# A decoder of two layers with routed experts: GpSimd makes the low halves of every fourth expert weight chunk

## The reference

```python
wg = w_gate.transpose(1, 0, 2).reshape(D, N_EXPERTS * EXPERT_HIDDEN)
wu = w_up.transpose(1, 0, 2).reshape(D, N_EXPERTS * EXPERT_HIDDEN)
wd = w_down.reshape(N_EXPERTS * EXPERT_HIDDEN, D)
h = jax.nn.silu(xc @ wg) * (xc @ wu)
h = (h.reshape(-1, N_EXPERTS, EXPERT_HIDDEN) * gc[..., None]).reshape(-1, N_EXPERTS * EXPERT_HIDDEN)
return h @ wd
```

## Time and profile before

| | |
|---|---|
| median of three runs | 2354.69 us |
| the profiled execution | 2358.64 us |
| its span (first to last instruction) | 2356.8 us |
| mean granted TensorE clock | 0.967 |
| first expert part (rows of experts 4 to 15) | 1436 to 1757 us |
| second expert part | 2016 to 2337 us |

### The profile page before, as it was taken

How to read it: one execution, slowest core, us unless ns; L and a number is a source line. 1 busy time by engine, 2 the same in 40 slices (tenths; PEclk the granted TensorE clock), 3 DMA queues, 4 the chain that set the end, 5 groups by cost and what they waited for, 6 DMA issues and landing times.

```text
span 2356.8 us, 36755 instructions
## 1 busy us (share of the span) xinstructions
PE 2232.4 (95%) x13894; PEld 1884.3 (80%) x13894; DVE 1489.5 (63%) x2333; ACT 1090.4 (46%) x1557; POOL 240.1 (10%) x241
## 2 busy tenths in 40 slices
PE   8999999999999999899999889999999898999997
PEld 6877667999787866799976579887888577888786
DVE  2946355755394635675534577888765267788876
ACT  1142452444114244244433355676654456666665
POOL 1914000100081400011000000000000000000000
PEclk9999899999999999999999889999999898999999
DMA  4432113555343221356532236888855414688883
GB/s 159 146 119 82 63 63 126 177 183 172 122 143 117 81 68 67 136 187 197 183 130 90 72 128 214 309 299 311 295 195 179 143 46 152 237 308 301 306 295 134
DMA packets 109808, 396.86 MB, mean 168 GB/s; under 512 B 12088, under 2 KB 14144, under 8 KB 109376
## 3 DMA queue, kind: packets, MB, share of 16 engines
q1 hardware_dynamic: 108576, 393.45, 49.0%
q10 hardware_dynamic: 1056, 1.06, 0.1%
HBM read 393.40 MB, written 1.06 MB: 167 GB/s over the span
## 4 chain that ended last, share of the span: by engine, by line
PE 81%; DVE 13%; ACT 4%; issue 2%; DMA 1%; DVEq 0%; SPq 0%; ACTq 0%
PE psum L544 79%; DVE W_LO L1690 3%; PE psum L552 1%; DVE region L1695 1%; DVE region L1698 1%; DVE RS L1727 1%; ACT region L1243 1%; ACT W_HI L1238 1%; DVE SQ L1695 1%; ACT region L1247 0%; DMA ring<-in_weights 0%; ACT SQ L1243 0%; DMA PAR<-in_params 0%; ACT L1243 0%; DVE X_LO L1695 0%
## 5 line engine op out<-in xcount | busy, mean ns | idle before, releaser
L1690 DVE TENSOR_TENSOR W_LO<-ring,W_HI 128x1024 fp32r<-128x1024 f32 x435 | 533.0, 1225 | 218.6 <-ACT W_HI L1238 208.5
L1238 ACT ACTIVATE W_HI<-ring 128x1024 fp32r<-128x1024 f32 x435 | 461.8, 1062 | 325.1 <-PE psum L544 245.6
L544 PE MATMUL psum<-HN,ring 128*128 128x272 f32 (+1 forms) x1728 | 411.9, 399 | 9.7 <-DVE HN L1702 9.7
L544 PEld LDWEIGHTS psum<-HN,ring 128*128 128x128 f32 x1728 | 332.2, 194 | 82.1 <-issue 16.6
L544 PE MATMUL psum<-X_HI,W_HI 128*128 128x256 f32 x808 | 232.3, 287 | 8.1 <-DVE W_LO L1690 6.6
L544 PE MATMUL psum<-X_LO,W_HI 128*128 128x256 f32 x808 | 227.6, 282 | 0.0
L544 PE MATMUL psum<-X_HI,W_LO 128*128 128x256 f32 x808 | 227.4, 281 | 0.0
L1247 ACT ACTIVATE region<-psum 128x272 f32<-128x272 f32 (+10 forms) x227 | 89.6, 395 | 280.0 <-PE psum L544 258.7
L1690 DVE TENSOR_TENSOR W_LO<-SQ,W_HI 128x1024 fp32r<-128x1024 f32 x128 | 156.8, 1225 | 37.0 <-ACT W_HI L1238 32.9
L544 PE MATMUL psum<-W_HI,XG_HI 128*128 128x512 f32 x384 | 152.9, 398 | 17.3 <-DVE W_LO L1690 15.3
L544 PE MATMUL psum<-FN_HI,W_HI 128*128 128x272 f32 (+1 forms) x592 | 169.2, 286 | 0.0
(11 more groups left out here) (328 smaller groups left out, 4203.1 us busy)
## 6 DMA issues: line engine op xcount, KB each, us to landing
ring<-in_weights SPq DMA_DIRECT2D x615, 512.0 KB, 4.1
SQ<-in_weights SPq DMA_DIRECT2D x128, 512.0 KB, 4.8
XT<-in_x SPq DMA_DIRECT2D x1, 1088.0 KB, 5.1
CST<-in_consts SPq DMA_DIRECT2D x1, 1082.5 KB, 7.3
SQ<-bias_by_distance ACTq DMA_DIRECT2D x1, 1024.0 KB, 5.3
out<-XT SPq DMA_DIRECT2D x8, 128.0 KB, 1.9
PAR<-in_params SPq DMA_DIRECT2D x1, 572.0 KB, 8.2
bias_by_distance<-MIX ACTq DMA_DIRECT2D x1, 12.0 KB
```

What stands on the lines that cost most here:

```text
L544: ins = nc.tensor.matmul(dst, w, x, start=start, stop=stop, skip_group_check=True)
L1238: lane(nc.scalar.activation(W_HI[:, s % SPLIT, :], ring_slot(n), ACT.Copy), split_hi)
L1690: lane(nc.vector.tensor_tensor(W_LO[:, s % SPLIT, :], ring_slot(n), W_HI[:, s % SPLIT, :].bitcast(F32), ALU.subtract), split_lo)
```

## The change

In the two expert parts the low half of a chunk with c = 3 (every fourth: the last of gate, up and down of each of 16 experts, in two layers, 96 in all) is made by GpSimd, with the same subtraction. It reports on a semaphore of its own, `split_pool`. TensorE and SyncE wait for that one where a chunk is GpSimd's. VectorE leaves these chunks out and keeps the order of all else; ScalarE's part is as before. GpSimd goes through the expert steps with `abreast` in the same way, three chunks ahead, and has nothing else to do there. TensorE gets one more wait per layer: ahead of the first chunk of expert 4 it waits until the last gathered pair of banks has been read.

```diff
+        self.by_pool = []
...
-            def chunk(split=False, routed=None):
+            def chunk(split=False, routed=None, by_pool=False):
...
-                    pe.wait_ge(split_lo, i + 1)
+                    splits.by_pool.append(by_pool)
+                    pe.wait_ge(split_pool if by_pool else split_lo, splits.by_pool.count(by_pool))
...
-                return chunk(True, (l, e // GROUP, at + c))
+                return chunk(True, (l, e // GROUP, at + c), by_pool=(at + c) % 4 == 3)
...
                 w = expert_chunk(l, part, e, c)
+                if (part, e, c) == ("gate", GROUP, 0):
+                    for p in range(2):
+                        banks.await_read(pe, ("gathered", l, p, KT - 1))
...
             def split(s, n):
 
+                if splits.by_pool[s]:
+                    return
                 dve.wait_ge(split_hi, s + 1)
...
         def _(pool):
             lane = Lane(pool, sem("gpsimd_step"))
 
+            def split(s, n):
+
+                if not splits.by_pool[s]:
+                    return
+                pool.wait_ge(split_hi, s + 1)
+                lane(nc.gpsimd.tensor_tensor(W_LO[:, s % SPLIT, :], ring_slot(n), W_HI[:, s % SPLIT, :].bitcast(F32), ALU.subtract), split_pool)
+
+            follow = Follower(splits, split)
+
+            def abreast(l, step):
+
+                follow.to(min(splits.marks[step][0] + SPLIT - 1, splits.first["moe", l, "last"] + 1))
+
+            def moe_done(l):
+                follow.to(splits.first["moe", l, "last"] + 1)
+                follow.ceilings.pop(0)
...
             for name, *args in SCHEDULE:
-                if name in steps:
+                if name in ("moe_lead", "wide", "rows", "rows_turn", "rows_down", "wide_down"):
+                    abreast(args[0], ("step", name, *args))
+                elif name in steps:
                     steps[name](*args)
+                follow(("step", name, *args))
...
                 if splits.before[n] is not None:
-                    split_, count = rank[splits.before[n]]
-                    sp.wait_ge(split_lo if split_ else w_used, count)
+                    sp.wait_ge(*rank[splits.before[n]])
```

More of the change, by code:

```diff
@@ L515, in build_program @@
         arrived = [sem(f"weights_arrived{s}") for s in range(ROUTED_RING)]
-        w_used, split_hi, split_lo, split_used = (sem(n) for n in ("weights_used", "split_hi", "split_lo", "split_used"))
+        w_used, split_hi, split_lo, split_pool, split_used = (sem(n) for n in ("weights_used", "split_hi", "split_lo", "split_pool", "split_used"))
         splits = Splits()
@@ L2468, in load @@
                 sp.dma_start(ring_slot(n), stream[bass.ds(row, 128), :]).then_inc(arrived[splits.slot[n]], 16)
-            split_chunks = set(splits.chunks)
-            rank, counts = [], [0, 0]
+            maker = {n: split_pool if by_pool else split_lo for n, by_pool in zip(splits.chunks, splits.by_pool)}
+            rank, counts = [], {}
             for n in range(n_chunks):
-                counts[n in split_chunks] += 1
-                rank.append((n in split_chunks, counts[n in split_chunks]))
+                freed = maker.get(n, w_used)
+                counts[freed.name] = counts.get(freed.name, 0) + 1
+                rank.append((freed, counts[freed.name]))
             group_at, begin = {}, {}
```

## The result

The changed kernel takes 2380.19 us (median of nine runs, 2372.37 to 2384.86) against 2358.25 us of the kernel before in nine runs (2348.59 to 2366.28). The ratio is 1.0091, 95% interval 1.0072 to 1.0109: slower by 22 us. I had forecast 2352 us and a range to 2371, so the time lies outside it, and on the other side.

A forecast was written before the change was run, and what follows sets the result against it. TensorE, 95% busy, was taken to bound the kernel, low halves giving back at most 15 us. Two layers of -2.7 us gain plus 1.3 us gate cost gave -2.8 us, predicting 2352 us, range 2340 to 2371.

The forecast's parts named there:

- the price of GpSimd's subtraction: Each moved low half: GpSimd's plain 128 x 1024 subtraction taken as 1.95 us, between 1.82 and 2.88.
- the 0.13 us a gate: Last chunk of some 10 of 12 row gates: ready after 4.24 us, wanted after 4.11; 1.3 us a layer lost.
- VectorE is shut out: VectorE instructions with two SBUF inputs wait for GpSimd's whole instruction; PSUM readers run free; no 1.25 us gained per chunk.
- the waits at u5.2, g6.0, d10.0 and g12.0: TensorE in full stretches: u5.2 0.7 us late, g6.0 0.25 earlier, d10.0 as late as before, g12.0 at 1630.1 instead of 1631.06.
- The slope: Each 0.1 us on GpSimd's instruction moves the sum about 2.8 us: 10 gates and 4 full-stretch places, in two layers.
- margin of 1.1: VectorE's low half of a row chunk: made in 3.0 us, needed after 4.11, so 1.1 us to spare.
- Rival 1: GpSimd's instruction is longer, uncovered at g.3 of every row expert: at 2.35 us +8.4, 2363 us; chance 0.27.
- sign of being wrong, a minimum above 2.1 us: In the profile, a minimum above 2.1 us for GpSimd's subtraction would refute the forecast in favour of rival 1.
- Rival 3: GpSimd gets in ahead of TensorE's next chunk more often, some two more a layer: +8 us, 2360 us; chance 0.13.
- The gain of 2.7 us a layer in the full stretches: Where VectorE is full, TensorE waits less: 0.25 us at e = 5, 1.77 at e = 8, 0.7 at e = 11.
- The new wait at g4.0: First chunk of expert 4: costs nothing, since XG_LO is done at 1435.68 and TensorE waits for SGM until 1435.93 anyway.
- SyncE's later ring slots: Ring slots behind GpSimd's chunks come free 0.7 us later; cost nothing, as ScalarE hardly waits for landings.

## Why the prediction was wrong

- **The step that failed is the price of GpSimd's subtraction: 1.95 us, where it takes 2.41.** I drew a line through squares, which read one tile twice, and a subtraction with broadcast inputs, whose two inputs are views of one tile as well (`HB`, L2440). The kernel that reads one tile twice shows 1.89 us, so that line was right for such inputs and not for this one. The trace had a nearer row, the convolution's sum of two different tiles:

```profile
L2428 POOL TENSOR_TENSOR region<-region x60: 763/900/905, 56.0 to 704.9; 128x272 f32<-128x272 f32 x60
```

  0.763 us at 272 columns stands against 0.641 for the square of the same size. The prediction doesn't weigh it. With the 0.18 us that the squares' line has at no columns, 0.763 gives (0.763 - 0.18) x 1024 / 272 + 0.18, about 2.37 us, an estimate from rows of before; the runs show 2.41. The Trainium skill (GPSIMD Engine Reference, "3.1 Elementwise — side-by-side cycle accounting") gives 4497 ns for 2048 columns; half of it, the estimate of 2.25 us in the prediction, was nearer than the 1.95 I took.
- **Up to the length it assumed, the mechanism and the total hold.** For 1.95 us the prediction has -1.4 us a layer; at 1.96 us the part is 1.6 shorter, at 1.89 us (-2.2 by its slope) 2.3. That the total came so near is partly luck: 0.6 of the 1.6 us is the wide chunks' pace, and the 0.13 us a gate never came, since the row gate of before begins g.3 4.22 us after g.0, not 4.11 (its first chunk takes 1.47 us). With 816 columns g.3 of the gates begins 4.21 to 4.22 us after g.0 too. VectorE is shut out as foreseen, PSUM readers run free, and the waits at u5.2, g6.0, d10.0 and g12.0 stand where they were drawn (0.38, 0.65, 1.34 and 1.01 us shown at 1.89 us).
- **The slope was half of what it is, and that is the second step that failed.** I had 2.8 us per 0.1 us for both layers. From 1.96 to 2.41 us the two parts grow by 27.8 us, 6.2 per 0.1 (some 2.4 of the 27.8 us is the wide chunks' pace). At the row gates a length of 2.41 gives 2.04 + 0.14 + 2.41 + 0.05 = 4.64 us, 0.42 over the 4.22; g.3 begins after 4.63 us, and 0.12 more is lost behind it. But new places join in, which the prediction put at nothing. (Of the other row chunks it says that most have a wide chunk among the three before them; GpSimd's wide chunks it doesn't price at all.) Two GpSimd chunks in a row need more than the pace gives (three wide downs, 1.06 us each by the starts), VectorE's next chunk after a shut-out of 2.1 us misses its margin of 1.1 (d6.2 and d9.2, 1.16 each), u4.3 costs 0.55, and the second matmul of six wide chunks 0.1 each. In the first layer that is 6.7 us; with the prediction's own sum for 2.41 us, +5.0, that makes about the +11.7 measured.
- **Rival 1 was the course**, by the right mechanism, but its sum for 2.41 us is +10 for both layers where +22 was measured, and it had 0.27. The prediction's sign of being wrong, a minimum above 2.1 us, was met: it is 2.38. Rival 3 (GpSimd gets in ahead more often) also came in part. The gain of 2.7 us a layer in the full stretches is not visible at 2.41: g6.0 and g9.0 wait half a microsecond less, u5.2 and u8.2 0.9 more.
- **The new wait at g4.0** costs nothing, as argued: 0.92 us for `SGM` before and after. SyncE's later ring slots show little: ScalarE's waits for ring landings are 79.0 us over the whole span against 73.5. No run tests what they cost.

## What to carry over

An instruction that moves to another engine is priced by the row with the same kind of inputs (same tile twice, broadcast, two different tiles), even if that row is disturbed: its minimum is then a better bound than a clean row of another kind. If the two engines exclude each other, work is not shared but queued: here 118 us of moved work lowered VectorE's busy time by 33 us. The moved piece then pays only where the other engine does something that doesn't wait for it, and only if it fits the tightest margin, the one behind another moved piece included. A short wait can cost twice what it shows (0.54 us for 0.26), so waits are priced by the distance between starts.

## What the runs showed of the hardware

- GpSimd's subtraction of 128 x 1024 float32 took 1.89 us where both inputs were the same tile, 2.41 us where they were two (2.43 for two other tiles); at 816 columns 1.96 us for two.
- A GpSimd fill (0.95 us for 128 x 1024) does not hold up VectorE's two-input instructions: their maximum was 1229 ns. By the Trainium skill (SBUF — State Buffer, "Who interferes with whom") only a GpSimd instruction that reads SBUF does; the runs agree.
- GpSimd's subtraction holds up the shorter multiply of `HE` by `GB` too, which has two SBUF inputs: it took 1350 ns on average in the part, against 692. `HE` from PSUM took 691 to 693 ns before and after.
- At a granted clock of 1.00 the matmuls of a wide chunk came 0.113 or 0.118 us apart, whole turns long, without a wait in the views. At 0.50 those of a row chunk came 0.43 us apart instead of 0.23.
